# MLP down projections by seven quarter products in place of eight

## What is computed

```python
D_MODEL = 1024; SEQ = 512; D_FF = 4 * D_MODEL

def squared_relu_mlp(h, w1, w2):
    return jnp.square(jax.nn.relu(h @ w1)) @ w2

# in each of the two layers
h = rms_norm(x, g[2])
x = x + rms_norm(squared_relu_mlp(h, mlp_w1[i], mlp_w2[i]), g[3])
```

## Time and profile before

| | |
|---|---|
| median of 3 runs | 1767.77 us (1765.96 to 1768.43) |
| span of the profiled execution | 1764.2 us (its time around the span is not listed) |
| TensorE busy | 1737.4 us, 8243 matmuls |
| weight loads busy | 1445.3 us |
| VectorE, ScalarE, GpSimd busy | 785.8, 662.9, 876.9 us |
| read from HBM | 153.10 MB |

### The profile page before, as it was taken

The page is one execution under the profiler, slowest core; times in us unless marked ns, Lnnn a source line. Parts: engine busy times, 40 slices in busy tenths (PEclk is TensorE's granted clock), DMA queues, the critical chain, the costliest instruction groups (busy, mean ns, idle before and its releaser), DMA issues.

```text
span 1764.2 us, 22985 instructions
## 1 busy us (share of the span) xinstructions
PE 1737.4 (98%) x8243; PEld 1445.3 (82%) x8243; DVE 785.8 (45%) x1225; ACT 662.9 (38%) x1039; POOL 876.9 (50%) x473
## 2 busy tenths in 40 slices
PE   8999999999999999999999999999999999999999
PEld 6887888888888877878888888889878888888887
DVE  6558654301331479956430133137856344444200
ACT  6338543312322456554321232135357332222221
POOL 3457545444444469755544444445445544444442
PEclk9999999999999999999999999999999999999999
DMA  5531123223333213123333332322210233332332
GB/s 190 133 98 59 37 72 107 95 95 96 96 96 99 80 48 108 60 84 95 103 99 96 96 95 95 95 84 72 87 49 14 95 95 96 97 101 98 96 107 71
DMA packets 46073, 158.45 MB, mean 90 GB/s; under 512 B 5744, under 2 KB 6000, under 8 KB 46000
## 3 DMA queue, kind: packets, MB, share of 16 engines
q1 hardware_dynamic: 46000, 157.45, 28.5%
HBM read 153.10 MB, written 2.10 MB: 88 GB/s over the span
## 4 chain that ended last, share of the span: by engine, by line
PE 90%; DVE 5%; ACT 2%; issue 1%; POOL 1%; DMA 0%; SPq 0%; DVEq 0%; POOLq 0%; ACTq 0%
PE PS L1834 26%; PE PS L1835 26%; PE PS L1836 26%; PE PS L1903 2%; DVE PS L1219 1%; PE PS L1939 1%; PE PS L1934 1%; PE PS L1935 1%; PE PS L2095 1%; PE PS L1844 1%; PE PS L1876 0%; PE PS L1976 0%; DVE PS L1211 0%; PE PS L2118 0%; PE PS L2119 0%
## 5 line engine op out<-in xcount | busy, mean ns | idle before, releaser
L548 POOL TENSOR_TENSOR wl<-raw,wh 128x1024 fp32r<-128x1024 f32 x216 | 523.0, 2422 | 623.2 <-ACT wh L742 198.3
L1835 PE MATMUL PS<-XLR,wh 128*128 128x512 f32 x1216 | 474.2, 390 | 0.0
L1834 PE MATMUL PS<-XHR,wh 128*128 128x512 f32 x888 | 348.8, 393 | 6.3 <-POOL wl L618 5.8
L1836 PE MATMUL PS<-XHR,wl 128*128 128x512 f32 x888 | 346.4, 390 | 0.0
L1834 PE MATMUL PS<-HH,wh 128*128 128x512 f32 x688 | 267.6, 389 | 0.0
L1835 PE MATMUL PS<-HL,wh 128*128 128x512 f32 x688 | 267.6, 389 | 0.0
L1836 PE MATMUL PS<-HH,wl 128*128 128x512 f32 x688 | 267.6, 389 | 0.0
L1835 PEld LDWEIGHTS PS<-XLR,wh 128*128 128x128 f32 x1216 | 229.1, 188 | 47.0
L728 ACT ACTIVATE wh<-raw 128x1024 fp32r<-128x1024 f32 x123 | 128.9, 1056 | 242.2 <-PE PS L1836 197.6
L1834 PEld LDWEIGHTS PS<-XHR,wh 128*128 128x128 f32 x888 | 167.4, 188 | 42.0 <-POOL wl L618 6.2
L1836 PEld LDWEIGHTS PS<-XHR,wl 128*128 128x128 f32 x888 | 167.4, 188 | 35.4
(11 more groups left out here) (344 smaller groups left out, 2561.6 us busy)
## 6 DMA issues: line engine op xcount, KB each, us to landing
raw<-weights SPq DMA_DIRECT2D x287, 512.0 KB, 3.5
X<-x_t SPq DMA_DIRECT2D x8, 256.0 KB, 6.7
out_t<-X SPq DMA_DIRECT2D x8, 256.0 KB, 4.7
KH<-rope_h SPq DMA_DIRECT2D x4, 128.0 KB, 4.7
KL<-rope_l SPq DMA_DIRECT2D x4, 128.0 KB, 5.5
QH<-XHR SPq DMA_DIRECT2D x16, 32.0 KB, 2.0
QL<-XLR SPq DMA_DIRECT2D x16, 32.0 KB, 2.0
pos_i<-positions SPq DMA_DIRECT2D x1, 256.0 KB, 8.5
```

The lines of the kernel that those rows point to most:

```text
L548: pool.tensor_tensor(wl[:, j], raw[:, j], wh[:, j].bitcast(F32), ALU.subtract).then_inc(w_lo, 1)
L1834: pe.matmul(out, wa, xa, start=start, stop=False)
L1835: pe.matmul(out, wa, xb, start=False, stop=False)
L1836: return pe.matmul(out, wb, xa, start=False, stop=stop)
```

## The change

The down projection is done by Winograd's form of Strassen's 2 x 2 scheme. A quad takes two output tiles and eight ff tiles, four even and four odd. Its weights are a 2 x 2 grid: row A1 the first output tile, row A2 the second, column 1 the even ff tiles, column 2 the odd ones, each entry half a block. The hidden values are a grid too: H1 the even ff tiles, H2 the odd ones, second index 1 the left 256 tokens, 2 the right 256. Sums of weights S1 = A21 + A22, S2 = S1 - A11, S4 = S2 - A12, S3 = A11 - A21 and sums of hidden values T1 = H12 - H11, T2 = H22 - T1, T3 = H22 - H12, T4 = T2 - H21 are formed. Seven products of 256 tokens follow in place of eight: A11 H11, S1 T1, A12 H21, S2 T2, S4 H22, A22 T4, S3 T3. Five additions (`read`) take them from PSUM into M, and `restore` turns a quarter's sign back at the end.

Chunks shrink from 16 to 8 ff tiles, four chunks a layer. The first up tile of the next chunk, the lead, is made before the quads of a chunk (four quads, `down_quads`). In the last chunk the outputs 6 and 7 are made as whole tiles, output 6 ahead of the three quads and output 7 behind them; output 7 takes its sum so far from M by two identity matmuls of 512 columns. That is 30 of 32 pairs by quads.

VectorE makes the four weight sums of a quad in two PSUM banks (`quad_sum`) and their low parts (`quad_low`); ScalarE makes all seven high parts (`quad_high`) in a ring of eight half blocks; GpSimd makes the low parts of A11, A12 and A22 (`quad_lows`). For each pair of ff tiles ScalarE makes the high parts of the hidden values and of their sums (`hidden_even`, `hidden_odd`, with `even_kept` a copy of the even tile for the sums), and VectorE the sums (`odd_sums`) and all low parts: `hidden_low` for the tiles, `sums_low` for the sums of a pair, which runs within the next even tile's `even_low`. The hidden parts lie in TH and TL, a ring of five pairs. The squares of the outputs move to ScalarE (`square_m`) and their additions to GpSimd (`add_output`), between the weights' lows.

The diff, cut to the parts named here:

```diff
-CHUNK = 16
+CHUNK = 8
 NCHUNK = FF // P // CHUNK
+HALF_S = S // 2
+QUADS = 4
+PRODUCTS = 7
+READS = 5
+LAST_PRODUCT = (0, 1, 4, 5, 6)
...
-    _PHASES += [(f"mlp0_up{_c}", CHUNK, CHUNK), (f"mlp0_down{_c}", 8 * CHUNK // SLOTS, 8)]
+_PHASES += [("mlp0_up0", CHUNK, CHUNK)]
+for _c in range(1, NCHUNK):
+    _PHASES += [(f"mlp0_lead{_c}", 1, 1), (f"mlp0_down{_c - 1}", KT, KT), (f"mlp0_up{_c}", CHUNK - 1, CHUNK - 1)]
...
+def quad_high(n0, h):
+    u, i = divmod(h, PRODUCTS)
+    q, n = QUAD0[n0] + u, n0 + 2 * u
+    if h < 8:
+        sc.wait_ge(blocks_done, n0 - RING + h // 2 + 1)
+    else:
+        sc.wait_ge(products_made, PRODUCTS * QUAD0[n0] + h - 8 + 1)
+    if i in (A11, A12, A22):
+        block, half = {A11: (n, 0), A12: (n, 1), A22: (n + 1, 1)}[i]
+        sc.wait_ge(raw_in[block % RING], 16 * (block // RING + 1))
+        x = raw_half(block, half)
+    else:
+        sc.wait_ge(quad_sums, 4 * q + {S1: 2, S2: 3, S4: 3, S3: 4}[i])
+        x = SUM_A if i in (S1, S4) else SUM_B
+    sc.activation(quad_weight(wh, n0, u, i), x, ACT.Copy).then_inc(quad_hi, 1)
+def mlp(layer, entry, job):
     boundary(entry, BLOCK0[f"mlp{layer}_up0"])
     enter(f"mlp{layer}_up0", entry)
+    def hidden_even(c, t):
+        T, p = up_block(layer, c, t)[1], 4 * c + t // 2
+        sc.wait_ge(bank_free, T + 1)
+        sc.activation(parts(TH, p, H11, 2), squared(0), ACT.Copy)
+        if p:
+            sc.wait_ge(sums_made, 4 * NCHUNK * layer + p)
+        sc.activation(even_kept[:], squared(0), ACT.Copy).then_inc(hid_hi, 1)
+    def hidden_odd(c, t):
+        p = 4 * c + t // 2
+        sc.wait_ge(sums_made, 4 * NCHUNK * layer + p + 1)
+        sc.activation(parts(TH, p, H21, 2), squared(1), ACT.Copy).then_inc(hid_hi, 1)
+        for i, half in ((H_T1, 0), (H_T4, 1)):
+            sc.activation(parts(TH, p, i, 2), t_sums[:, S * half:S * half + S], ACT.Copy).then_inc(sums_hi, 1)
...
+        n0, _, quads = down_block(layer, c)
+        for t in range(1 if c else 0, CHUNK):
+            n = up_block(layer, c, t)[0]
+            if n >= n0 - RING:
+                quad_high(n0, 2 * (n - n0 + RING))
+                quad_high(n0, 2 * (n - n0 + RING) + 1)
+            elif c or t >= 4:
+                hi(n + RING)
+            if t % 2:
+                hidden_odd(c, t)
+            else:
+                hidden_even(c, t)
+            if layer == 0 and c < 2 and t == 3:
+                sc.wait_ge(dw_low_done, 1)
+                low_taps(c)
+        for h in (6, 7):
+            quad_high(n0, h)
+        if c < NCHUNK - 1:
+            hidden_even(c + 1, 0)
+            for h in range(8, PRODUCTS * quads):
+                quad_high(n0, h)
+            for j in range(RING):
+                hi(n0 + 2 * quads + j)
...
+def quad_sum(n0, u, i):
+    q, n = QUAD0[n0] + u, n0 + 2 * u
+    if i == S1:
+        v.wait_ge(raw_in[(n + 1) % RING], 16 * ((n + 1) // RING + 1))
+        tt(SUM_A, raw_half(n + 1, 0), raw_half(n + 1, 1), ALU.add).then_inc(quad_sums, 1)
+    elif i == S2:
+        v.wait_ge(raw_in[n % RING], 16 * (n // RING + 1))
+        v.wait_ge(quad_sums, 4 * q + 1)
+        tt(SUM_B, SUM_A, raw_half(n, 0), ALU.subtract).then_inc(quad_sums, 1)
...
+    def hidden(c, t):
+        n, T = up_block(layer, c, t)
+        z = PS[:, T % 4]
+        v.wait_ge(blocks_done, n + 1)
+        step(tt(tmp[:, 0], z, r2[:], ALU.mult))
+        stt(squared(t), z, 0.0, tmp[:, 0], ALU.max, ALU.mult).then_inc(bank_free, 1 + SKIP.get(n, 0))
+        v.wait_ge(bank_free, T + 1)
+    even, odd = squared(0), squared(1)
+    def hidden_low(p, i, x, n):
+        done = 2 * (4 * NCHUNK * layer + p) + n
+        v.wait_ge(hid_hi, done)
+        sig(tt(parts(TL, p, i, 2), x, f(parts(TH, p, i, 2)), ALU.subtract), hid, done)
+    def sums_low(p):
+        done = 2 * (4 * NCHUNK * layer + p)
+        for i, half in ((H_T1, 0), (H_T4, 1)):
+            v.wait_ge(sums_hi, done + half + 1)
+            tt(parts(TL, p, i, 2), t_sums[:, S * half:S * half + S],
+               f(parts(TH, p, i, 2)), ALU.subtract).then_inc(sums_lo, 1)
+    def even_low(c, t):
+        p = 4 * c + t // 2
+        hidden_low(p, H11, even, 1)
+        if p:
+            sums_low(p - 1)
+            v.wait_ge(sums_lo, 2 * (4 * NCHUNK * layer + p))
+        step(tt(t_sums[:, 0:HALF_S], even[:, right], even_kept[:, left], ALU.subtract))
+    def odd_sums(c, t):
+        t1, t3, t4, t2 = [t_sums[:, i * HALF_S:(i + 1) * HALF_S] for i in range(4)]
+        tt(t3, odd[:, right], even_kept[:, right], ALU.subtract)
+        step(tt(t2, odd[:, right], t1, ALU.subtract))
+        sig(tt(t4, t2, odd[:, left], ALU.subtract), sums_made, 4 * NCHUNK * layer + 4 * c + t // 2 + 1)
+    def odd_low(c, t):
+        hidden_low(4 * c + t // 2, H21, odd, 2)
...
-        with v.Fori(0, CHUNK // 4, 1) as g:
-            for j in range(4):
-                z, x = PS[:, (T0 + j) % 4], squared(j)
-                v.wait_ge(blocks_done, g * 4 + (n0 + j + 1))
-                tt(tmp[:, 0], z, r2[:], ALU.mult).then_inc(dve, 1)
-                v.wait_ge(dve, g * 4 + (base + j + 1))
-                stt(x, z, 0.0, tmp[:, 0], ALU.max, ALU.mult).then_inc(bank_free, 1)
-                v.wait_ge(hid_hi, g * 4 + (h0 + j + 1))
-                tt(HL[:, g * 4 + j], x, f(HH[:, g * 4 + j]), ALU.subtract).then_inc(hid, 1)
-                v.wait_ge(hid, g * 4 + (h0 + j + 1))
-        for m in range(KT - 1):
-            T = T0 + m
-            v.wait_ge(blocks_done, n0 + 2 * m + 2)
+        last = c == NCHUNK - 1
+        n0, T0, quads = down_block(layer, c)
+        for t in range(1 if c else 0, CHUNK):
+            hidden(c, t)
+            if t == 6:
+                quad_low(n0, 0, S1)
+                quad_sum(n0, 0, S4)
+            if t % 2 == 0:
+                even_low(c, t)
             else:
-                v.tensor_copy(M[:, m], PS[:, T % 4]).then_inc(bank_free, 2)
-                v.wait_ge(bank_free, T + 2)
-    last_output(out_job, T0 + KT - 1)
+                odd_sums(c, t)
+                if t == CHUNK - 1:
+                    quad_low(n0, 0, S2)
+                    quad_sum(n0, 0, S3)
+                odd_low(c, t)
+            if t == 4:
+                quad_sum(n0, 0, S1)
+                quad_sum(n0, 0, S2)
+        if last:
+            v.wait_ge(blocks_done, n0)
+            sums_low(4 * NCHUNK - 1)
+            sig(tt(M[:, KT - 2], M[:, KT - 2], PS[:, (T0 - 1) % 4], ALU.add), bank_free, T0)
+            quad_low(n0, 0, S4)
+        else:
+            hidden(c + 1, 0)
+            quad_low(n0, 0, S4)
+            even_low(c + 1, 0)
+        for u in range(quads):
+            more = u + 1 < quads
+            if more:
+                quad_sum(n0, u + 1, S1)
+            quad_low(n0, u, S3)
+            read(c, u, 0)
+            if more:
+                quad_sum(n0, u + 1, S2)
+            read(c, u, 1)
+            if last and u:
+                restore(u - 1, READS * (QUAD0[n0] + u))
+            if more:
+                quad_low(n0, u + 1, S1)
+                quad_sum(n0, u + 1, S4)
+                quad_low(n0, u + 1, S2)
+            read(c, u, 2)
+            if more:
+                quad_sum(n0, u + 1, S3)
+            read(c, u, 3)
+            if more:
+                quad_low(n0, u + 1, S4)
+            read(c, u, 4)
...
-        n0, T0 = BLOCK0[f"mlp{layer}_down{c}"], TILE0[f"mlp{layer}_down{c}"]
-        for m in range(KT):
-            open_tile(T0 + m)
-            last = m == KT - 1
-            out = PS[:, RB if last else (T0 + m) % 4]
-            for b in range(2):
-                open_block(n0 + 2 * m + b)
-                if m == 0:
-                    pe.wait_ge(hid, h0 + SLOTS * (b + 1))
-                for k in range(SLOTS):
-                    x = SLOTS * b + k
-                    ins = products(out, *weight(n0 + 2 * m + b, k), HH[:, x], HL[:, x],
-                                   x == 0 and (c == 0 or not last),
-                                   x == CHUNK - 1 and (c == NCHUNK - 1 or not last))
-                ins.then_inc(blocks_done, 1)
...
+        for k in range(QUADS):
+            slot, p = 4 * (at_half % 2) + k, (4 * c + k) % H_RING
+            ins = products(out, wh[:, at_half // 2, slot], wl[:, at_half // 2, slot],
+                           TH[:, p, operand], TL[:, p, operand], k == 0, k == QUADS - 1)
+        ins.then_inc(products_made, 1)
...
+    def down_quads(c):
+        first, second = slice(0, HALF_S), slice(HALF_S, S)
+        for u in range(down_block(layer, c)[2]):
+            product(c, u, A11, open_bank(c, u, 0)[:, first], H11)
+            product(c, u, S1, open_bank(c, u, 1)[:, first], H_T1)
+            y, z = open_bank(c, u, 2), open_bank(c, u, 3)
+            product(c, u, A12, y[:, first], H21)
+            product(c, u, S2, z[:, second], H_T2)
+            product(c, u, S4, y[:, second], H22)
+            product(c, u, A22, z[:, first], H_T4)
+            product(c, u, S3, open_bank(c, u, 4)[:, first], H_T3)
...
```

(14 more changed lines are left out.)

362 lines of the change are left out of this document (279 added, 83 removed).

## The result

| | before | after |
|---|---|---|
| median of the runs | 1767.18 us (4 runs) | 1838.22 us (4 runs, 1836.52 to 1839.88) |
| ratio | | 1.0404, 95% interval 1.0389 to 1.0418 |
| span of the profiled execution | 1764.2 us | 1836.1 us |

A forecast was written before the change was run, and what follows sets the result against it. TensorE, busy 98% of the span, was taken to bound the kernel. Turns 56.4 + last chunks 8.0 + clock 13.2 - gain 27.3 = +50.3 us: 1814.5 on the span, 1818 with 3.6 added for the median; range 1780 to 1858.

The forecast's parts named there:

- six turns: From up to down, three a layer: TensorE stands until VectorE has made the last pair's low sums; 56.4 us in all.
- last chunks: Each layer's last chunk: TensorE waits for hidden low parts, sum lows and the last block's low part; 4.0 a layer, 8.0 us.
- clock: Behind each of the six turns the granted clock falls to 0.50, losing 2.2 us each; 13.2 us.
- gain of the quads: Down projection: 84 narrow matmuls replace 48 wide ones, 0.94 us less per quad, thirty quads; net gain 27.3 us.
- they just miss: VectorE's two-SBUF operations (low sums, S1, S3) would not meet GpSimd's work; a meeting would cost up to 1.8 us more.
- Turn hidden: Rival, chance 0.06: at the turns the pair's sum lows are ready when the lead tile ends; -19.3 us, 1748.
- VectorE keeps up: Rival, chance 0.14: VectorE never lags, so turns cost 4.98 us only; +20 us, 1788.
- the clock does not fall: Rival, chance 0.07: the clock stays up behind the turns; +37 us, 1805.
- steps as long as in the old loop: Rival, chance 0.20: VectorE's steps take 0.82 and 0.73 us; +75 us, 1842, or 1861 with the quads' 19 on top.
- extra price of 0.8 a quad: Inside quads: at the longer VectorE steps it takes 10.8 us against TensorE's 9.96; 19 us in 24 quads.

The follow-up runs named there:

- low sums first: Changed kernel, with VectorE making the low parts of the last pair's sums ahead of the lead tile's hidden work, not behind it: 1824.9 us.
- S3 late: Changed kernel with the last pair's low sums ahead of the lead's hidden work and, except in the last chunk, weight sum S3 behind it: 1814.9 us.
- no meeting at the entry: Changed kernel, with GpSimd holding the fifth up tile's weight low part in each layer's first chunk until VectorE has made the second pair's low sums: 1838.5 us.
- filled turns: Changed kernel, with TensorE filling the six turns from up to down with 512-column matmuls that have no use: 1824.6 us.
- S2 late: Changed kernel, with S2's high part in tile 6 put behind the even tile's two copies in ScalarE's queue: 1822.9 us.

## Why the prediction was right, and where its sizes were off

The direction, the mechanism and every place that the sum names held; "the rest" had no term in it. The terms, in us on the profiled span:

| term | forecast | measured |
|---|---|---|
| six turns | 56.4 | 62.1 |
| last chunks | 8.0 | 8.6 |
| clock | 13.2 | 15 |
| gain of the quads | -27.3 | -23.7 |
| the rest | 0 | 9.9 |
| sum | 50.3 | 71.9 |

**Turns.** The steady ones were forecast to 0.05 us (5.8 against 5.85). The second of layer 0 was 1.6 longer than forecast, the first ones 1.7 and 2.2. In layer 1 the eight tiles of VectorE took 4.82, 4.12, 5.17, 4.13, 7.78, 4.12, 7.09 and 4.75, forecast 3.85, 4.08, 5.17, 4.08, 6.49, 4.08, 7.10 and 4.63. Two are off. Tile 0 is late by 1.0 because two weight copies stand ahead of its copies on ScalarE. Tile 4 is late by 1.3 because its low sums met GpSimd (VectorE's row, then GpSimd's):

```profile
906.86 2.51 DVE L1423 TENSOR_TENSOR TL<-sqb,TH 128x512 fp32r<-128x512 f32 x2
...
904.72 2.40 POOL L623 TENSOR_TENSOR wl<-raw,wh 128x1024 fp32r<-128x1024 f32 x1 [12.61 <-ACT wh L870]
907.08 1.74 POOL L685 TENSOR_TENSOR wl<-raw,wh 128x512 fp32r<-128x512 f32 x1
```

That is the term of the turns that the prediction had wrong: it named this cost with up to 1.8 us, put it at nothing and said "by my times they just miss". They met at the fifth tile of each layer. They met again at tile 4 of layer 0's second chunk, beside GpSimd's operations of 390.93 (2.40 us) and 394.74 (1.29 us), which is 1.5 of the 1.6 us at that turn: the low sums took 1.84 where 1.29 is usual, S1 1.62 where 0.70 is:

```profile
392.64 1.84 DVE L1423 TENSOR_TENSOR TL<-sqb,TH 128x512 fp32r<-128x512 f32 x2
...
394.97 1.62 DVE L1423 TENSOR_TENSOR PS<-raw 128x512 f32<-128x512 f32 x1
```

The runs with low sums first, with S3 late and with no meeting at the entry show how one place more or less decides it.

**Clock.** The forecast had six falls of 2.2 us. The trace has eight, of 1.5 to 2.4: the last chunks' pair of waits, 1.78 and 1.44 us, costs one too. The six at the turns make 12.4, and the run with filled turns took 12.6 off behind the input stage.

**Gain.** A narrow step is 0.1200 us over whole stages, where seven steps of the earlier trace rows gave 0.1186; a quad is 10.08 us, the gain 0.82. The earlier trace rows gave 0.120 already, though for 264 columns. A load lasts 200 ns here beside these steps of 120 ns, so loads run beside matmuls. The list in the Trainium skill by which a load overlaps matmuls only where the row groups differ (page "TensorE: Matmul & The Clock Gate", Part 3, "The mechanism") isn't borne out, as the prediction expected from the earlier trace rows.

**The rest.** 3.3 us lie ahead of the change, in the input stage: in the profiled execution after, the granted clock was 0.50 from 12 to 18 us, before it was 1.00. 1.5 more lie behind the last MLP. The other 5 us, in the layers, are several: 0.65 is the lead's wait for its weights in layer 0; the rest I have not separated.

**The rivals.** "Turn hidden" and "VectorE keeps up" fell with the turns' rows, "the clock does not fall" with the windows, "steps as long as in the old loop" because no wait stands in a quad and the tiles took the short steps. 1838 lies near that last rival's 1842, for another reason. Its extra price of 0.8 a quad is too low by its own steps: 4 x 0.82 + 9 x 0.73 + 1.2 is 11.05, which is 1.1 above 9.96.

## What to carry to other kernels

Fewer multiplications on the engine that bounds a kernel are paid for by the engines that make the sums: count those engines' time tile by tile up to the place where the bounding engine must wait, and there look at what stands ahead in their queues. Ask of each such operation which engine has room for it; here the same low parts on GpSimd made the kernel 50 us shorter than on VectorE, though the steady turns still waited 1.60 us for them. An edit that shortens a wait on a full engine comes back as waits elsewhere until work is taken off it.

## What the runs showed of the hardware

- At the upper clock a matmul's step is longer than its columns take; at the lower level it isn't. 0.2136 us for 256 columns at 1.2 GHz is 256/1.2 but for 0.0003, and 0.1200 at 2.4 GHz is 0.0133 over 256/2.4. For 512 columns 0.2271 is 0.0138 over 512/2.4. The two agree with a fixed time of some 13 ns a matmul; the 264 columns of the earlier trace rows, 0.0100 over 264/2.4, agree less well. By it a quad's 36 more matmuls take 0.5 us off the 1.36 us that an eighth of 10.90 would be. The Trainium skill (page "TensorE: Matmul & The Clock Gate", section "Wait — 56ns, not 53.3ns?") states such a cost, with 2.5 ns; the measured 13 ns decide here.
- Halving the columns once more would gain little, by this estimate: in the kernel before, eight matmuls of two columns, each with a weight load of its own, take 0.81 us up to the next one's start, 0.10 each, not much less than the 0.1200 for 256 columns:

```profile
1206.43 0.95 PE L2264 MATMUL PS<-headones,head_q 128*128 128x2 f32 x8
1207.24 0.37 PE L1903 MATMUL PS<-XHR,wh 128*128 128x264 f32 x1
```

  What sets that pace is not shown.
- Whether the clock falls isn't told by the waits alone. In the last chunk of the kernel after it was 0.50 behind the waits of 1.78 and 1.44 us (a window):

```profile
598.80:600.80 2.00, 2.00 (x9) 2.00 (x10) 1.93 (x3) 0.63 (x1) 0.73 (x2) 0.50 0.98 383
```

  It was 1.00 where the wait of 1.78 was gone and that of 1.44 was left (the same place in the kernel with S2 late):

```profile
594.90:596.90 2.00, 1.97 (x16) 1.98 (x17) 1.93 (x3) 0.63 (x1) 0.71 (x2) 1.00 0.98 342
```

  But it was 1.00 as well in the second layer of the kernel with low sums first, where both waits stand:

```profile
1195.86:1197.86 2.00, 2.00 (x16) 2.00 (x17) 1.93 (x3) 0.63 (x1) 0.72 (x2) 1.00 0.97 381
```

  Of the twelve last chunks with both waits, in six kernels, eleven had the fall; of the two with the wait of 1.44 alone, none. In the kernel with S3 late it fell behind a wait of 1.88 us in the first layer and not behind the two of 1.87 in the second. What decides it is not shown.
